# A hybrid retention, short-convolution and FFN layer on eight cores: closing norms reordered, operands of a small product swapped, loads of the second tile moved

## The reference

```
h   = rms_norm(x, pre_mix_w);  p = h @ w_in          # q k v g | B C hc, 7 x 512 columns
ret = silu(g) * head_norm(retention(rot(q), rot(k), v))
cnv = B * causal_dwconv3(C * hc)
x   = x + rms_norm(concat[ret, cnv] @ w_out, post_mix_w)
h2  = rms_norm(x, pre_ffn_w)
f   = (gelu(causal_dwconv3(h2 @ w_up)) * (h2 @ w_gate)) @ w_down      # 4096 FFN columns
x   = x + rms_norm(f, post_ffn_w)                     # y
```

## Time and profile before

| | us |
|---|---|
| three runs, slowest core | 2037.8, 2044.03, 2418.83 (median 2044.03) |
| profiled execution | 2035.24 |
| its span, slowest core (4) | 2033.7 |
| spans of all cores | 2012.9 to 2033.7 |
| PE busy / DVE / ACT / POOL | 1968.1 / 1282.0 / 976.9 / 479.8 |

### The profile page before, as it was taken

One profiled execution on the slowest core, in us unless ns is written; L12 is line 12 of the kernel. 1 busy time (PEld: TensorE's weight loads), 2 busy tenths in 40 slices (PEclk: granted clock), 3 DMA queues, 4 the chain that ended last, 5 costly groups with the idle time before them and its releaser, 6 DMA issues.

```text
span 2033.7 us, 29432 instructions; the slowest of 8 cores (2012.9 to 2033.7 us)
## 1 busy us (share of the span) xinstructions
PE 1968.1 (97%) x10630; PEld 932.1 (46%) x10630; DVE 1282.0 (63%) x2317; ACT 976.9 (48%) x1929; POOL 479.8 (24%) x1031
## 2 busy tenths in 40 slices
PE   6998999999999999999999999999999999999997
PEld 3454444444544444444444444444444444444443
DVE  6677756668568655674656836668356755567445
ACT  6576784753444453444533444434534445334323
POOL 4654100102332421113211223104221132111001
PEclk9999999999999999999999999999999999999999
DMA  9946878976445544463435643446443544435332
GB/s 283 263 145 189 272 230 262 280 258 243 168 166 193 206 145 165 156 199 140 165 134 176 207 151 114 173 149 227 141 163 130 195 175 139 157 131 191 135 134 107
DMA packets 109522, 368.97 MB, mean 181 GB/s; under 512 B 8904, under 2 KB 43552, under 8 KB 97216
## 3 DMA queue, kind: packets, MB, share of 16 engines
q1 hardware_dynamic: 109104, 366.98, 53.2%
q10 hardware_dynamic: 272, 0.10, 0.0%
HBM read 313.43 MB, written 53.62 MB: 180 GB/s over the span
## 4 chain that ended last, share of the span: by engine, by line
PE 83%; DMA 8%; DVE 3%; ACT 3%; issue 1%; SPq 1%; POOL 0%; POOLq 0%; DVEq 0%; ACTq 0%
PE pF L903 33%; PE pF L962 20%; PE pM L713 9%; PE pM L752 7%; PE pM L851 5%; DMA wug<-wug_s 2%; DMA x_sb<-xp 2%; DMA wug<-w_in 2%; PE pM L903 1%; PE pT L634 1%; PE pM L962 1%; PE pF L713 1%; DMA v_sb<-w_down 1%; PE pT L657 1%; PE pF L752 1%
## 5 line engine op out<-in xcount | busy, mean ns | idle before, releaser
L903 PE MATMUL pF<-hT,wug 128*128 128x512 bf16 x3840 | 864.0, 381 | 16.2 <-DMA wug<-wug_s 7.1
L903 PEld LDWEIGHTS pF<-hT,wug 128*128 128x128 bf16 x3840 | 371.4, 98 | 455.5 <-DVE act L914 8.6
L962 PE MATMUL pF<-wdn,act 128*128 128x512 bf16 x1840 | 419.2, 379 | 7.4 <-DVE act L914 5.5
L906 ACT ACTIVATE up_sb<-pF 128x512 f32<-128x512 f32 x240 | 142.6, 594 | 347.0 <-PE pF L903 343.3
L962 PEld LDWEIGHTS pF<-wdn,act 128*128 128x128 bf16 x1840 | 177.9, 98 | 221.1 <-issue 7.3
L909 DVE SCALAR_TENSOR_TENSOR acc<-up_sb,cvec,acc 128x512 f32<-128x512 f32 x256 | 191.1, 747 | 134.6 <-ACT acc L908 134.4
L914 DVE TENSOR_TENSOR act<-pF,gl 128x512 bf16<-128x512 f32 x229 | 157.7, 689 | 139.5 <-ACT gl L913 124.3
L907 POOL COPY halo_f<-up_sb 128x2 f32<-128x2 f32 x256 | 70.2, 274 | 652.5 <-ACT up_sb L906 651.9
L913 ACT ACTIVATE gl<-acc 128x512 bf16<-128x512 f32 x256 | 159.8, 625 | 103.3 <-DVE acc L911 102.8
L713 PE MATMUL pM<-slab,hT 128*128 128x512 bf16 x856 | 199.5, 382 | 4.6 <-ACT slab L581 3.8
L911 DVE SCALAR_TENSOR_TENSOR acc<-up_sb,cvec,acc 128x512 f32<-128x512 f32 x256 | 198.7, 776 | 5.2
(11 more groups left out here) (368 smaller groups left out, 2256.2 us busy)
## 6 DMA issues: line engine op xcount, KB each, us to landing
wug<-wug_s SPq DMA_DIRECT2D x208, 512.0 KB, 3.9
wdn<-wdn_s SPq DMA_DIRECT2D x28, 2048.0 KB, 8.0
slab<-slab_s SPq DMA_DIRECT2D x54, 1024.0 KB, 5.4
x_sb<-xp SPq DMA_DIRECT2D x32, 512.0 KB, 8.0
stg<-w_up SPq DMA_DIRECT2D x32, 512.0 KB, 10.1
wug_s<-wug SPq DMA_DIRECT2D x32, 512.0 KB, 9.5
yp<-x_sb SPq DMA_DIRECT2D x32, 512.0 KB, 9.3
stg<-w_in SPq DMA_DIRECT2D x18, 512.0 KB, 10.0
```

The costliest lines, as they stand in the source:

```text
L903: op("pe", [lambda e, k=k, u=u, pp=pp: e.matmul(pp[:, :nt], lhsT=wug[:, sl, u, k, :], rhs=hT[:, k, :nt], start=(k == 0), stop=(k == 7)) fo ...
L906: op("act", lambda e: e.activation(out=upv[:, 2:2 + nt], in_=PU[:, :nt], func=AF.Copy), [RU, RUP], [RUP], c_act(nt))
L962: op("pe", [lambda e, q=q, hs=hs, m=m, cols=cols, pd=pd: e.matmul(pd[:m, :], lhsT=al[q][0][:, cols], rhs=wdn[:, cs_[q] % 8, hs], start=(q ...
```

## The change

1. post: the product with the weight no longer waits for the rms. gw multiplies source and weight; after pow, gx does out * rms + x in one instruction. For the last 128 rows of tile 8 everything runs in halves of 512 columns: square, sum, product, addition and an output DMA each.
2. down_s: for tile 0, wdn is stationary (128 x 128) and 16 columns of act move, 64 matmuls per group into one bank, summed in faF (part of Pm). After the last group: transposition, copy, DMA to fs_s in DRAM, DMA back as rows into tmpA, post.
3. x of tile 2 gets a lead of -9 and less (was 4 and less).
4. The planner starts its engines at 1.05 and its DMA at 2.55 us, and counts 1.3 us for ACT's first table load.
5. The two DMAs of T1 get a semaphore key of their own, "cst1".

The rest gives names to orders of steps; FIRST, LATER, JOINT and T2_F0 hold the orders that were there before, and the other branches ("woven", "ret+out" and so on) are not reached.

```diff
+SLAB_1 = 2
+X1_LEAD = (130.0, 31.0, 29.0, 28.0)
+X2_LEAD = -9.0
+T_START = 1.05
+T_TABLE = 1.3
+GROUP_KEYS = ("cst", "cst1", "so")
...
-        free = {e: 0.0 for e in engs}
+        free = {e: T_START for e in engs}
...
-        dma_t = 0.0
+        dma_t = T_START + 1.5
...
+                if e == "act" and not table:
+                    table = True
+                    st += T_TABLE
...
-    dma(T1[0:96, :], ffn_cw..., ("cst",), 49152, eng="act")
-    dma(T1[96:108, :], conv_w..., ("cst",), 6144, eng="act")
+    dma(T1[0:96, :], ffn_cw..., ("cst1",), 49152, eng="act")
+    dma(T1[96:108, :], conv_w..., ("cst1",), 6144, eng="act")
...
-    lead=... 4.0 - s if tl["t"] == 2 else (130.0, 31.0, 29.0, 28.0)[s])
+    lead=... X2_LEAD - s if tl["t"] == 2 else X1_LEAD[s])
...
+        gw = lambda hs: op("dve", lambda e: e.tensor_tensor(out=out_ap[:, hs], in0=src_ap[:, hs], in1=wb_tile[:m, hs], op=ALU.mult),
+                           src_of(hs) + [wb_key], out_of(hs), ...)
+        gx = lambda hs: op("dve", lambda e: e.scalar_tensor_tensor(out=x_sb[:m, xs_, hs], in0=out_ap[:, hs], scalar=ra, in1=x_sb[:m, xs_, hs], op0=ALU.mult, op1=ALU.add),
+                           out_of(hs) + [RS, ("x", xs_)], ...)
...
+        if part is None:
+            sq(whole, ssa)
+            op("dve", ... out=aa, in0=ssa, scalar1=1.0 / D, scalar2=EPS ...)
+            op("pool", ... out=ra, in0=aa, in1=negh[:m, 0:1], op=ALU.pow ...)
+            gw(whole)
+            gx(whole)
+        else:
+            sq(halves[0], ssa)
+            op("dve", ... out=aa, in0=ssa ...)
+            gw(halves[0])
+            sq(halves[1], sa2)
+            op("dve", ... out=a2, in0=sa2, scalar=1.0 / D, in1=aa ...)
+            op("pool", ... out=ra, in0=a2, ... op=ALU.pow ...)
+            gw(halves[1])
+            for q, hs in enumerate(halves):
+                gx(hs)
+                part(q, hs)
...
+    def down_s(tl, cs_, g):
...
+        op("pe", [lambda e, q=q, j=j: e.matmul(pd[:, j * DEC:(j + 1) * DEC], lhsT=wdn[:, cs_[q] % 8, j * 128:(j + 1) * 128], rhs=al[q][0],
+                                               start=(q == 0), stop=(q == n - 1)) for j in range(8) for q in range(n)],
+           [a[1] for a in al] + [("wdn", c % 8) for c in cs_], [RD], 8 * n * 0.029)
+        if start:
+            op("act", ... out=faF, in_=pd[:, 0:128], func=AF.Copy ...)
+        else:
+            op("dve", ... out=faF, in0=faF, in1=pd[:, 0:128], op=ALU.add ...)
+        if last:
+            op("pe", lambda e: e.transpose(out=pt[:, 0:128], in_=faF, identity=ident_f), ...)
+            op("act", ... out=tT, in_=pt[:, 0:128], func=AF.Copy ...)
+            dma(fs_s.rearrange("j t d -> (j t) d"), tT, [("fs", 1)], [("fs_s",)], ("fst",), 65536, lead=10.0)
+            dma(fa.rearrange("t (j d) -> t j d", j=8), fs_s.rearrange("j t d -> t j d"), [("fs_s",)], RF, ("fst2",), 65536, lead=10.0)
+            post(fa, RF, fa, RF, stat_f, "sf", 4, 0, DEC, wb_post_ffn, ("wb_post_ffn",), junk, [("junk",)], 8)
+            dma(ys, x_sb[:DEC, 8, :], [("x", 8)], [], ("y", 8), DEC * 4096)
...
     def down(tl, cs_, g):
+        if tl["t"] == 0:
+            return down_s(tl, cs_, g)
...
+                end = tl["t"] == 8 and s == 3
+                part = lambda q, hs: dma(tl["ydst"][s][:, hs], x_sb[:m, tl["slots"][s], hs], [("xh", q)], [], ("y", 9 + q), m * 2048)
```

More of the change, by code:

```diff
@@ L35 @@
 UG_ACT = (1, 3)
-G_FIRST = (2, 0, 1, 3)
-G_LATER = (0, 1, 2, 3)
-UG_LEAD = 8.0
-GROUP_KEYS = ("cst", "so")
+FIRST = (2, 0, 1, 3, "hc+ret", "b", "out")
+LATER = (0, 1, 2, 3, "hc+ret", "b", "out")
+SLAB_1 = 2
+T2_F0 = tuple(range(0, 32, 2))
+JOINT = (1, 2, 0)
+UG_LEAD = 8.0
+X1_LEAD = (130.0, 31.0, 29.0, 28.0)
[3 more added lines that the diff above has]
+GROUP_KEYS = ("cst", "cst1", "so")
 C_MM = 0.2165
@@ L647, in post @@
         RS = ("st" + sk[1], c)
[L648 to L652, removed]
@@ L653, in post @@
[L653 to L654 removed]
+        gw = lambda hs: op("dve", lambda e: e.tensor_tensor(out=out_ap[:, hs], in0=src_ap[:, hs], in1=wb_tile[:m, hs], op=ALU.mult),
+                           src_of(hs) + [wb_key], out_of(hs), 0.15 + 0.00106 * (hs.stop - hs.start))
+        gx = lambda hs: op("dve", lambda e: e.scalar_tensor_tensor(out=x_sb[:m, xs_, hs], in0=out_ap[:, hs], scalar=ra, in1=x_sb[:m, xs_, hs], op0=ALU.mult, op1=ALU.add),
+                           out_of(hs) + [RS, ("x", xs_)], [("x", xs_)] if part is None else [("xh", hs.start // 512)], 0.15 + 0.0011 * (hs.stop - hs.start))
@@ L673, in mixer, with normed_once, ret_all @@
                 dma(cs[:, 0:ns], rot_s[:, tab0:tab0 + ns], [("rot_s", n) for n in range(tab0, tab0 + ns)], [("cs", "A")], ("cs",), ns * 65536, lead=20.0)
[L674 to L684, removed]
+        seq = FIRST if first else LATER
+        normed = []
+        def normed_once():
+            if not normed:
+                normed.append(1)
+                return True
+            return False
+        def ret_all(tl, conv=None):
             if tl["t"] == 0:
@@ L696, in mixer @@
                 dma(srp.rearrange("h d e -> d h e"), S2[:, 0], [("S", 0, h) for h in range(H)], [], ("so", "p0"), 262144)
[L697 to L705, removed]
+        so = []
+        for step in seq:
+            if step in (0, 1, 2, 3):
+                sl = load_slab(first, step)
+                once = normed_once()
+                for tl in tls:
+                    for s in range(tl["ns"] if once else 0):
+                        norm(tl, s)
+                    for s in range(tl["ns"]):
+                        tok_group(tl, step, sl, s)
+            elif step == "hc":
+                sl_hc = load_slab(first, 6)
+                sl_c = load_slab(first, 5)
+                once = normed_once()
+                for tl in tls:
+                    for s in range(tl["ns"] if once else 0):
+                        norm(tl, s)
+                    for j in range(4):
+                        conv_in(tl, j, sl_hc, sl_c)
+            elif step == "hc+ret":
+                sl_hc = load_slab(first, 6)
+                sl_c = load_slab(first, 5)
+                for tl in tls:
+                    ret_all(tl, (sl_hc, sl_c))
+            elif step == "b":
+                sl_b = load_slab(first, 4)
+                for tl in tls:
+                    for j in range(4):
+                        conv_out(tl, j, sl_b)
+            elif step == "ret":
+                for tl in tls:
+                    ret_all(tl)
+            elif step == "out":
+                so = [load_slab(first, 7), load_slab(first, 8)]
+                for tl in tls:
+                    for s in range(tl["ns"]):
+                        out_proj(tl, s, so)
+                        norm(tl, s, True)
+            elif step in ("woven", "woven2"):
+                one, two, dec = tls
+                sl_hc = load_slab(first, 6)
+                sl_c = load_slab(first, 5)
+                for q in range(4):
+                    ret_a(one, q)
+                    for tl in (one, two, dec):
+                        conv_in(tl, q, sl_hc, sl_c)
+                    ret_b_part(one, q)
+                sl_b = load_slab(first, 4)
+                for tl in tls:
+                    for j in range(4):
+                        conv_out(tl, j, sl_b)
+                        if step == "woven2" and tl is two:
+                            ret_a(two, j)
+                            ret_b_part(two, j)
+                so = [load_slab(first, 7), load_slab(first, 8)]
+                for q in range(4):
+                    if step == "woven":
+                        ret_a(two, q)
+                    out_proj(one, q, so)
+                    norm(one, q, True)
+                    if step == "woven":
+                        ret_b_part(two, q)
+                ret_all(dec)
+                for tl in (two, dec):
+                    for q in range(tl["ns"]):
+                        out_proj(tl, q, so)
+                        norm(tl, q, True)
+            elif step == "ret+out":
+                so = [load_slab(first, 7), load_slab(first, 8)]
+                for tl in tls:
+                    ret_all(tl)
+                    for s in range(tl["ns"]):
+                        out_proj(tl, s, so)
+                        norm(tl, s, True)
@@ L1021, in build_program @@
     wide[0] = True
-    mixer([tiles[1], tiles[2], tiles[0]], 0)
+    mixer([tiles[t] for t in JOINT], 0)
     P.handover(keys("qT", "B") + keys("kT", "B") + keys("kte", "B") + keys("v_sb", "B"), wdn_keys)
@@ L1055, in build_program @@
     act_free[:] = [k for k in act_free if k < NACT]
-    ffn([(tiles[2], range(1, 32, 2))], 1)
+    ffn([(tiles[2], [c for c in range(32) if c not in T2_F0])], 1)
     P.handover([("act", NACT + q) for q in range(4)], keys("qT", "A"))
```

52 lines of the change are left out of this document (40 added, 12 removed).

## The result

The median is 2020.8 us (2016.5 to 2021.2, four runs); before, beside it, 2042.0. The ratio is 0.9907, with a 95% interval of 0.9893 to 0.992: 19 us (16 to 22) faster, which is less than 2%, so the verdict is "same". The forecast was 2027 with -10.9 us.

A forecast was written before the change was run, and what follows sets the result against it. PE, busy 97% of the span, was taken as the bound. Terms -6.8 - 1.4 + 2 - 1 - 3.2 - 0.5 = -10.9 us, from 2037.8, gave a forecast of 2027 us, range 2013 to 2043.

The forecast's parts named there:

- the fourth rival: At the start: the new order also takes PE's idle time and the w_out wait, 7 us better, 2020; chance 0.12.
- 16 tokens, PE time (-6.8): Tile 0's down product: four groups each 1.79 us shorter on PE, less one 0.41 us transposition, net -6.8 us.
- rivals: 1: Casting stage: PE time won in three groups is given back waiting at the next cast, 5.4 us, 2032; chance 0.17.
- 2 for all four groups: Rival at the four small-matmul runs: the clock falls to its lower level behind them, +6.8 us, 2034; chance 0.09.
- Bank wait and fs_s (-1.4 + 2 = +0.6): Last 16-token group: a 1.44 us bank wait goes; the path through fs_s holds tmpA, costing 2 us.
- The third rival: Third tile's first products: fs_s path frees tmpA later than about 510, PE stands, +15 instead of +2, 2040; chance 0.15.
- Closing norms off the tail (-1): Closing norms before the tail: shorter chain and banks let go without the rms save 1 us, bounds -3.5 and +1.
- Tail (-3.2): Behind PE's last product: earlier last accumulation and halved norm end the span 3.2 us sooner, bounds -5 and -1.
- pow (+0.5): In the tail: pow on POOL slows beside a DVE instruction with two SBUF inputs, costing 0.5 us.
- Start (-0.5): At the start: x of tile 2 behind the second slab wins some PE idle time, -0.5 us, bounds -4 and +4.

The follow-up runs named there:

- e4: The kernel before with only the new start (x of tile 2 later, planner start times, constants' key): ratio 1.0003, 2043.37 us.
- e1: The changed kernel run again with no edit: 2022.31 us, ratio 0.9914 to the kernel before.
- e7: The changed kernel with the old start (x of tile 2, planner start times, constants' key) put back: ratio 0.9927 to the kernel before.
- e9: The changed kernel with the last norm whole instead of in halves: ratio 0.9921 to the kernel before.
- e12: The changed kernel with the old start and the last norm whole instead of in halves: ratio 0.9919 to the kernel before.
- e13: The changed kernel with the old start, last norm in halves, its second square under its own key: ratio 0.9905 to the kernel before.
- e2: The kernel before with only the 16 tokens' product turned round (old norms, old start): ratio 0.9998, 2043.35 us.
- e6: The changed kernel with the old closing norms put back, so the 16 tokens and the new start: ratio 1.0014 to the kernel before.
- e3: The kernel before with only the closing norms changed, the last one in halves: ratio 0.9951, 2031.03 us.
- e5: The changed kernel with the 16 tokens' product as before, so new norms and new start: ratio 0.9934 to the kernel before.

## Why the prediction was right, and by how much it was off

The side and the bound (PE, then what takes its place) were right; 2020.8 lies in the range, and the gain is 1.7 times the forecast. The time stands at the number of the fourth rival (2020), but not by its mechanism: a, which holds PE's idle time in the first mixer, is 17.3 us before and after, and the start alone is 1.0003. (Its 7 us were also more than the two rows that it names, 2.8 and 2.3.) Taking the two kernels without any effect (before, e4) against the six with all that counts (after, e1, e7, e9, e12, e13), the mean span falls by 2026.4 - 2010.2 = 16.1 us: PE work -10.3, c -4.1, tail -3.0, a -0.4, b +1.3, clock +0.3. By the steps:

- **16 tokens, PE time (-6.8).** Right in kind, somewhat small. I set a duration (1.76) against a start to start time (3.55); the start to start time of the new form is 1.62, so four groups less 0.1 for the transposition are -7.6. The table has -7.8 to -10.4 in its four like pairs (before and e2, e4 and e6, e3 and e7, e5 and after); no row shows what the part beyond -7.6 is. The forecast read the section "Wait — 56ns, not 53.3ns?" of the Trainium skill's "TensorE: Matmul & The Clock Gate" too narrowly: besides 62 ns per MATMUL with hardware decode off it gives a floor of about 25 ns from start to start for small ones, and 1.62 us here, 25 ns per matmul, agrees with that floor.
- **That the parts can be summed.** This failed. By itself the gain of the 16 tokens is 0, since idle time and the low clock take all of it; it is 5 us only with the new norms. I had both mechanisms as rivals: 1 for the three groups inside the casting stage, where column a does not rise, and 2 for all four groups. With the old norms they struck behind the fourth group only, where the next mixer's norm feeds PE, and at 628 us, where no rival had looked; in the changed kernel neither place has them.
- **Bank wait and fs_s (-1.4 + 2 = +0.6).** Like kernels with and without the 16 tokens differ in b by +2.3 us (2.2 and 2.3 against 4.4 to 4.9). tmpA came at 510.7, at the late end of 501 to 511, as the write took 9.4 us to land, more than the 7.2 us of ys (7.0 to 9.8 by core; the read back 3.8 to 5.6). PE stood for 2.7 us in all, and half of the cores show one low clock stretch there. So the size of the +2 is right, but the wait is another: 2.5 us are for act, behind the 16-token norm in DVE's order, and only 0.2 us for the bank behind tmpA. The third rival's point (510) was reached, its price (+15) not: PE's list held more than the 5 us of work that it counted on, 40 FFN products (8.80 us at 496.14) alone.
- **Closing norms off the tail (-1).** The term that was most undersized: c falls by 4 us. I asked only who waits for a norm's bank and rms, and left the largest row, 7.1 us for wug, without a cause. It goes with the FFN norms (7.1 to 2.0 us on the cores of the pages; behind 560 us, as a mean over cores, 4.5 to 0.7 us between the two kernels and the six).
- **Tail (-3.2).** Measured -2.7 (12.3 to 9.6). The last accumulation is where the sum had it, 0.4 us behind PE. The last addition ends 5.8 us behind PE, not 5.0, since the second square waits for L677 through the shared key, which I had read past, and pow takes 0.93 us. The cut, which I had counted as a gain, costs 0.6 us.
- **pow (+0.5).** Right, and everywhere: 1.46 us in the median of all FFN closings, 0.55 in those of the mixers, where the product reads PSUM:

```profile
L671 POOL TENSOR_TENSOR stat_m<-stat_m,negh x33: 538/548/1539, 161.3 to 1786.5; 128x1 f32<-128x1 f32 x32, 16x1 f32<-16x1 f32 x1
L671 POOL TENSOR_TENSOR stat_f<-stat_f,negh x32: 545/1460/2122, 464.9 to 2008.6; 128x1 f32<-128x1 f32 x31, 16x1 f32<-16x1 f32 x1
```

  That agrees with the Trainium skill's "SBUF — State Buffer" ("Who interferes with whom"), by which a DVE instruction with two SBUF inputs contends with a GpSimd instruction that reads SBUF, and one with at most one does not; the holding of the ports for a whole instruction, of which the forecast speaks, it states for another mode of DVE. Outside the tail I count it at nothing, as the product has to be done before the rms is of use anyway; no run took it alone.
- **Start (-0.5).** Nothing that shows: 1.0003 alone, and beside the rest all intervals overlap (e5 and e3, e6 and e2, after and e7, e9 and e12).

What stays open: how much of the norms' -10 us comes from the shorter chain, how much from the lists that the planner makes with it, and how much from the outputs' place in SP's queue. All three change together with the FFN closings. That a single lucky list made the gain is unlikely: three different lists with the 16 tokens and the old FFN norms all gave 0.9998 to 1.0014, and six with the new ones all gave 0.9905 to 0.9929.

## What to carry to other kernels

Work taken off a full engine need not show up at the end: here it did only where the next norm was ahead of PE. Test such an edit together with the one that loosens its feeders, as alone it can read as worthless. A row of waits without a named cause is a term of the sum, also when the edit does not touch its line: here output stores share the queue with the prefetches. And read the dependency keys of a piece before counting on its halves to overlap.

## What the runs showed that I had not expected

- 64 matmuls of 16 columns, each with its own 128x128 weights, took 1.62 us up to the next work: 25 ns each, less than the row's own length (1.76 us) says.
- A write of 64 KB to DRAM, issued at 490.45 with weight loads behind it, took 9.4 us to land (6.2 to 11.6 us over all cores with this write), although its issue takes 0.32 us, and the read back could only be issued then.
- The clock fell on 22 of 24 cores when the 64 small matmuls and 8 transpositions were followed by 2.1 to 2.8 us of idleness, and on none of the 47 cores where dense products stood between and PE did not wait for a slab either.
